# Sixteen of the 128 weighted expert sums of tile 0, moved from TensorE to VectorE

## What is computed

```python
wgt = softmax(best_s) * gelu(h . u[expert])      # 128 weights per token
out = sum over the 128 experts of wgt * v[expert]  # v[expert]: 1024 numbers
x = x + gate2 * out                                # then the last norm
```

## Time and profile before

| | us |
|---|---|
| median of 3 runs (lowest, highest) | 1479.16 (1478.48, 1480.18) |
| the profiled execution on the device | 1486.33 |
| its span, first to last instruction | 1484.4 |
| TensorE busy / VectorE / ScalarE / GpSimd | 1354.0 / 841.1 / 292.7 / 429.6 |
| gathers | 256, 268.48 MB, 43.7% of the DMA engines' span |
| mean granted TensorE clock | 0.983 |

### The profile page before, as it was taken

The page is one execution under the profiler, slowest core; times in us unless marked ns, Lnnn a source line. Parts: engine busy times, 40 slices in busy tenths (PEclk is TensorE's granted clock), DMA queues, the critical chain, the costliest instruction groups (busy, mean ns, idle before and its releaser), DMA issues.

```text
span 1484.4 us, 14879 instructions
## 1 busy us (share of the span) xinstructions
PE 1354.0 (91%) x5314; PEld 872.2 (59%) x5314; DVE 841.1 (57%) x1997; ACT 292.7 (20%) x690; POOL 429.6 (29%) x545
## 2 busy tenths in 40 slices
PE   7999999999999999999988989998989778778776
PEld 6887888898767777667566554444543222222222
DVE  3558451235127667524256567776766767666654
ACT  2023101031010000114423214541221112111101
POOL 0002000120101000000004544564557555655551
PEclk9999999999999999999898998999999999999999
DMA  8343633311557888537339998999999999999995
GB/s 293 115 170 114 227 114 113 120 51 57 171 186 282 309 297 293 204 127 284 113 114 364 423 422 332 395 421 424 424 424 425 425 425 425 425 426 424 425 425 229
DMA packets 119193, 424.52 MB, mean 286 GB/s; under 512 B 10642, under 2 KB 34632, under 8 KB 84176
## 3 DMA queue, kind: packets, MB, share of 16 engines
q0 software_dynamic: 36896, 268.48, 43.7%
q1 hardware_dynamic: 82224, 155.09, 29.0%
HBM read 422.48 MB, written 1.06 MB: 285 GB/s over the span
## 4 chain that ended last, share of the span: by engine, by line
PE 54%; DMA 26%; issue 7%; POOL 7%; ACT 3%; DVE 3%; SPq 0%; POOLq 0%; DVEq 0%; ACTq 0%
PE psum L560 30%; DMA arena<-peer_uv,arena 15%; DMA wr<-peer_uv,arena 7%; PE psum L811 4%; PE psum L1027 3%; POOL wr L2397 3%; POOL arena L2369 2%; DMA xc<-peer_uv,arena 2%; PE psum L787 2%; PE psum L881 1%; PE psum L857 1%; POOL arena L2397 1%; PE psum L608 1%; PE psum L998 1%; PE psum L1045 1%
## 5 line engine op out<-in xcount | busy, mean ns | idle before, releaser
L560 PE MATMUL psum<-hT,wr 128*128 128x256 f32 x1792 | 393.6, 382 | 1.6 <-DVE hT L1583 1.6
L560 PEld LDWEIGHTS psum<-hT,wr 128*128 128x128 f32 x1792 | 342.3, 191 | 51.9 <-issue 5.3
L1027 PE MATMUL psum<-wr,arena 128*128 128x512 f32 x644 | 312.2, 616 | 54.0 <-POOL arena L2369 53.8
L2215 DVE CUSTOM_DVE_ANT_0 wr<-psum,wr 128x1024 f32<-128x1024 f32 x161 | 196.9, 1223 | 148.4 <-DMA wr<-peer_uv,arena 148.3
L1027 PEld LDWEIGHTS psum<-wr,arena 128*128 128x128 f32 x644 | 114.1, 193 | 232.5 <-issue 232.1
L2397 POOL DMA_INDIRECT wr<-peer_uv,arena x161 | 160.8, 999 | 270.0 <-DVE arena L2163 125.4
L1027 PE MATMUL psum<-arena 128*128 128x512 f32 x276 | 135.3, 617 | 27.3 <-POOL arena L2369 27.0
L2369 POOL TENSOR_SCALAR arena<-cst,arena 128x128 f32<-128x128 f32 x256 | 121.8, 476 | 124.7 <-ACT arena L1431 117.1
L1431 ACT ACTIVATE arena<-arena 128x1 f32<-128x1 f32 x256 | 51.0, 202 | 492.8 <-DVE arena L2215 492.3
L1027 PEld LDWEIGHTS psum<-arena 128*128 128x128 f32 x276 | 48.0, 192 | 112.6 <-issue 112.4
L2215 DVE CUSTOM_DVE_ANT_0 arena<-psum,arena 128x1024 f32<-128x1024 f32 x69 | 84.5, 1224 | 50.2 <-DMA arena<-peer_uv,arena 50.1
(11 more groups left out here) (321 smaller groups left out, 1458.7 us busy)
## 6 DMA issues: line engine op xcount, KB each, us to landing
wr<-in_w_in SPq DMA_DIRECT2D x22, 2048.0 KB, 8.4
arena<-in_w_ada SPq DMA_DIRECT2D x12, 2048.0 KB, 9.8
wr<-in_w_up SPq DMA_DIRECT2D x22, 1024.0 KB, 8.0
arena<-piece SPq DMA_DIRECT2D x16, 1024.0 KB, 9.1
wr<-in_w_down SPq DMA_DIRECT2D x5, 2048.0 KB, 9.2
wr<-in_w_a_out SPq DMA_DIRECT2D x2, 2048.0 KB, 8.1
wr<-in_w_b_out SPq DMA_DIRECT2D x2, 2048.0 KB, 8.3
wr<-in_w_o SPq DMA_DIRECT2D x2, 2048.0 KB, 7.7
```

The costliest lines, as they stand in the source:

```text
L560: mm = nc.tensor.matmul(bank[p % 4][:, f * S:(f + 1) * S], slot(i)[:, k, c:c + P], act[:, k, :], start=k == 0, stop=k == KT - 1)
L1027: mm = nc.tensor.matmul(bank[(6, 0)[t] + half][:, :], diag[:, n % DIAGS, :], gring[slot_of][:, D + half * BANK:D + (half + 1) * BANK], sta ...
L2215: V.tensor_tensor_reduce(gring[slot_of][:, 0:D], h2[t], gring[slot_of][:, 0:D], 1.0, 0.0, ALU.mult, ALU.add, dots[:, t, c:c + 1]).then_inc ...
```

## The change

Sets 8, 14, 20, ... 98 (every sixth, 16 in all) get no diagonal and no matmuls. Three sets later, behind the dot of set n + 3, VectorE forms the product of the two weights (128x1) and adds weight times v to a sum in SBUF, `row_sum` (the first time it only writes it). The slot's next gather waits for that (`row_used`). At set 164 VectorE adds `row_sum` to banks 6 and 7 and then goes on as before. The counts of `diag_done` and `pe_used` go by the sets left on TensorE. The room for `row_sum` comes from the `C_SEL` blocks: the table is 1024 columns narrower, and L952 reads one column of the identity 128 times in their place. Every diagonal waits for `norm_done`, not only the first of each 16.

```diff
@@ constants
-C_SEL = C_NEG + NT * S
-C_IOTA = C_SEL + H * P
+C_IOTA = C_NEG + NT * S
...
-    for h in range(H):
-        t[h, C_SEL + h * P:C_SEL + (h + 1) * P] = 1.0
...
+ON_VECTOR = tuple(range(8, 104, 6))
+
+
+def on_tensor(n):
+
+    return n - sum(m < n for m in ON_VECTOR)
...
+        row_sum = sb("row_sum", [P, D])
+        row_weight = sb("row_weight", [P, 1])
@@ tensor
-                        mm = nc.tensor.matmul(o[:, c], cst[0:H, C_SEL + h * P:C_SEL + (h + 1) * P], small[:, 6, 0:n],
+                        mm = nc.tensor.matmul(o[:, c], cst[0:H, C_ID + h:C_ID + h + 1].to_broadcast([H, P]), small[:, 6, 0:n],
                                               start=False, stop=True, skip_group_check=True)
...
+                    if n in ON_VECTOR:
+                        continue
...
-                    pe.wait_ge(s["diag_done"], n + 1)
+                    pe.wait_ge(s["diag_done"], on_tensor(n) + 1)
                     for half in range(2):
-                        mm = nc.tensor.matmul(bank[(6, 0)[t] + half][:, :], diag[:, n % DIAGS, :],
+                        mm = nc.tensor.matmul(bank[(6, 0)[t] + half][:, :], diag[:, on_tensor(n) % DIAGS, :],
@@ vector
+            def vector_sum(n):
+
+                t, c = divmod(n, P)
+                dve.wait_ge(s["gelu_done"], n + 1)
+                chain.wait()
+                chain(V.tensor_tensor(row_weight[:, :], wgt[:, t, c:c + 1], gsoft[:, t, c:c + 1], ALU.mult))
+                chain.wait()
+                row = gring[GATHER[n][0]][:, D:2 * D]
+                i = ON_VECTOR.index(n)
+                if i == 0:
+                    V.tensor_scalar(row_sum[:, :], row, row_weight[:, 0:1], None, ALU.mult).then_inc(s["row_used"], 1)
+                else:
+                    dve.wait_ge(s["row_used"], i)
+                    V.scalar_tensor_tensor(out=row_sum[:, :], in0=row, scalar=row_weight[:, 0:1], in1=row_sum[:, :],
+                                           op0=ALU.mult, op1=ALU.add).then_inc(s["row_used"], 1)
+
+            def add_rows():
+
+                dve.wait_ge(s["pe_used"], on_tensor(P))
+                dve.wait_ge(s["row_used"], len(ON_VECTOR))
+                for n in range(2):
+                    c = slice(n * BANK, (n + 1) * BANK)
+                    V.tensor_tensor(bank[6 + n][:, :], bank[6 + n][:, :], row_sum[:, c], ALU.add).then_inc(s["rows_added"], 1)
...
                     if n == P + 36:
-                        gated_add(0, "pe_used", (P, P), 3, "x_final", (6, 7))
+                        add_rows()
+                        gated_add(0, "rows_added", (1, 2), 3, "x_final", (6, 7))
...
+                    if n - 3 in ON_VECTOR:
+                        vector_sum(n - 3)
@@ gpsimd
             def expert_diagonal(n):
 
+                if n in ON_VECTOR:
+                    return
                 t, c = divmod(n, P)
-                if n >= DIAGS:
-                    pool.wait_ge(s["pe_used"], n - DIAGS + 1)
-                if c % PK == 0:
-                    pool.wait_ge(s["norm_done"], n // PK + 1)
+                i = on_tensor(n)
+                if i >= DIAGS:
+                    pool.wait_ge(s["pe_used"], i - DIAGS + 1)
+                pool.wait_ge(s["norm_done"], n // PK + 1)
...
-                if before is not None:
-                    pool.wait_ge(s["pe_used"], before + 1)
+                if before in ON_VECTOR:
+                    pool.wait_ge(s["row_used"], ON_VECTOR.index(before) + 1)
+                elif before is not None:
+                    pool.wait_ge(s["pe_used"], on_tensor(before) + 1)
```

More of the change, by code:

```diff
@@ L114 @@
 wout_ready x3_done best_done soft_done eid_done gelu_done dot_done
-wuk_zero norm_done diag_done pe_used half_done x_final final_done h2_done""".split()
+wuk_zero norm_done rows_added diag_done pe_used row_used half_done x_final final_done h2_done""".split()
 class Chain:
@@ L2310, in _ @@
                 if n:
-                    dve.wait_ge(s["pe_used"], SETS)
+                    dve.wait_ge(s["pe_used"], on_tensor(SETS))
                 chain(V.tensor_tensor(gated[:, n, :], bank[n][:, :], modb[:, 3, c], ALU.mult))
@@ L2361, in expert_diagonal @@
             def expert_diagonal(n):
+                if n in ON_VECTOR:
+                    return
                 t, c = divmod(n, P)
-                if n >= DIAGS:
-                    pool.wait_ge(s["pe_used"], n - DIAGS + 1)
-                if c % PK == 0:
-                    pool.wait_ge(s["norm_done"], n // PK + 1)
+                i = on_tensor(n)
+                if i >= DIAGS:
+                    pool.wait_ge(s["pe_used"], i - DIAGS + 1)
+                pool.wait_ge(s["norm_done"], n // PK + 1)
                 pool.wait_ge(s["gelu_done"], n + 1)
-                G.tensor_scalar(diag[:, n % DIAGS, :], ident, wgt[:, t, c:c + 1], gsoft[:, t, c:c + 1], ALU.mult,
+                G.tensor_scalar(diag[:, i % DIAGS, :], ident, wgt[:, t, c:c + 1], gsoft[:, t, c:c + 1], ALU.mult,
                                 ALU.mult).then_inc(s["diag_done"], 1)
```

## The result

| | median | lowest to highest | runs |
|---|---|---|---|
| before | 1483.38 us | 1478.48 to 1486.97 | 19 |
| changed | 1488.34 us | 1482.23 to 1493.38 | 19 |

The ratio is 1.0032, 95% interval [1.0019, 1.0045]: by it the changed kernel is 4.7 us slower (the two medians differ by 5.0). The forecast was 3.6 us faster, with a range of up to 1481.5 against a median of 1479.16; on that scale the result is 1483.9. A second measurement of the same kernel gave 1.0031 [1.0012, 1.0051].

What follows compares the result with a forecast made beforehand. Bound by full DMA queues from 820 us, except 891 to 941, where gathers wait for TensorE's sums. Terms -7.2 + 3.6 = -3.6 us gave 1475.6 us against a median of 1479.16; range 1470 to 1481.5.

Steps and rivals of the forecast that it cites:

- The first term: At 891 to 941 us, relieved TensorE lets gathers issue earlier: 7.2 us recovered, ends 0 and 10.3.
- the hole: Stretches 891 to 916 and 916 to 941 us, at 337 and 334 GB/s: 10.3 us of transfer time lost.
- The second term: After 941 us, late vector-summed slots lose 0.75 us at each of gathers 57, 63, 69, 75, 81: 3.6 us.
- the steps of 3.2 us: Sign of being right: dots at 57, 63, 69, 75, 81 about 3.2 us apart, 2.49 between.
- the 390 GB/s in the hole: Sign of being right: 891 to 941 us runs at over 390 GB/s.
- The bound of 7.2: Upper end, in us, of the loss at the five gathers behind vector sums after 941 us; lower end 0.
- Rival 3: Slower: in GpSimd's one queue the vector sum comes late after 941 us; +7 us, 1486, chance 0.14.
- Its point of decision: Rival 3 decides if a sum is done 3 us later than reckoned: lead 1.5, 2.0 us lost per gather.
- Its formula: Into an empty queue a gather takes 6.0 us from issue to dot, so lead L loses 6.0 - 2.5 - L.
- The vector sum's own price: On VectorE behind dot b + 3: 0.16 and 1.28 us; slot free 2.9 us after that dot's start.
- Constants and broadcast weights: Smaller constant table: 0, or a gain of 1.2 us if exposed; weights read 128 times: old 0.19 us a load.
- VectorE's hold on GpSimd: Two-input vector sums lengthen GpSimd issues: at most 12 us over 16 sets, 0 on the path.

Runs made afterwards that it cites:

- e12_again: The changed kernel measured once more, nothing altered; 1.0031 of the kernel before.
- e3_relief: The changed kernel without vector sums: 16 of tile 0's 128 experts left out, their slots free with the dot; 0.9994 of the kernel before.
- e5_early: The changed kernel with the vector sum behind the dot of set n + 1 instead of n + 3; 1.0007 of the kernel before.
- e7_both: e5_early with the diagonal of set b + 2 laid before the wait for vector-summed set b; 1.0015 of the kernel before.
- e13_all: e7_both with ScalarE's copy before unit 0 of tile 1 waiting for the gelu of an earlier set; 1.0002 of the kernel before.
- e15_second: The changed kernel with the vector sum behind the dot of set n + 2 instead of n + 3; 0.9977 of the kernel before.
- e18_second_again: e15_second measured once more, nothing altered; 0.9978 of the kernel before.
- e4_hold: The kernel before with narrower constants, all sums on TensorE; sixteen gathers also wait for the third dot behind their slot's own; 1.0010 of the kernel before.
- e14_hold4: As e4_hold, but the sixteen gathers wait for the fourth dot behind their slot's own; 1.0146 of the kernel before.
- e2_load: The kernel before with narrower constants plus VectorE's sixteen operation pairs on `row_sum` alone, all sums on TensorE, no slot held; 1.0020 of the kernel before.
- e9_psum: e2_load with the long VectorE operation taking one input from PSUM instead of two from SBUF; 1.0001 of the kernel before.
- e8_fill: e3_relief with four zero-weight matmuls, waiting for no diagonal, in place of each dropped sum; 1.0004 of the kernel before.

## Why the prediction was wrong

**The first term, 7.2 us recovered, failed.** Its start came true: in the changed kernel's profile TensorE doesn't stand idle before unit 0 and comes at full clock, and gather 37 goes 3.2 us earlier, counted from dot 12 (forecast: 1.8; 1.2 in e12_again, which stands idle 1.4 us there). Gather 45 went at 913.24 where 914.8 was forecast, but that is luck, since this execution had started 4.0 us better; counted from dot 12 the gather is 4.0 us earlier than before, and 6.4 were forecast. The step that failed is "TensorE then has no 3.54 us to stand idle and keeps its clock ... By set 45 TensorE is 6 us ahead". It took TensorE as the only late one and the wait before unit 0 as its only wait. One step on, in the same unit, TensorE of the changed kernel stands 3.09 us (2.9 in e12_again) until VectorE has masked the logits, where before it stood 0.38:

```profile
884.52 0.70 PE L956 MATMUL psum<-arena 64*128 64x256 f32 x2
...
900.71 1.09 PE L971 MATMUL psum<-cst,arena 128*128 128x128 f32 x4 [3.09 <-DVE amax L2031]
901.59 2.97 PE L1036 MATMUL psum<-xc,arena 128*128 128x512 f32 x4
```

The sum behind it takes 2.97 us and not 1.88, the clock in the two halves of the hole is no better than before (0.89 and 0.90 for 0.88 and 0.93), and gather 49 is back at its old place (0.4 us later, counted from dot 12; in e12_again 0.2 earlier). In e3_relief the wait before unit 0 is longer, 6.68 us, and the full relief of 31 us, with no vector sum at all, gives 0.9994, at best 0.9976. TensorE's attention steps wait for ScalarE and VectorE, whose gelus and dots wait for the gathers. In the three kernels with the late slot the stretch from dot 12 to 49 is 115.9, 116.9 and 118.2 us, mean 117.0, against the 117.1 of the unrelieved kernels: nothing recovered, with an uncertainty of about 1. In the five with an earlier slot (e5_early, e7_both, e13_all, e15_second, e18_second_again) the mean is 115.3: 1.8 us less. But e4_hold, with no relief, has 115.3 too, so even this isn't told from nothing.

**The second term, 3.6 us at the gathers 57 to 81, was too small, and put in the wrong place.** A lead of 4.5 was forecast, and 4.5, 5.2, 4.6 and 4.7 stand in the trace. That the late slot would cost time was right. But the price was taken as 0.75 us at each of these gathers (five of them make 3.8, not 3.6), and their own dots lose 0.2, 0, 1.1 and 0 us, in e12_again nothing at all. The loss falls on the gathers behind them, such as 64 and 65 with 1.2 us each, which wait for TensorE. The term left that out: what a held gather does to the diagonals and sums behind it, and to the clock. Of the signs named, the steps of 3.2 us did not come at these sets (2.7, 2.5, 3.6 and 2.4), nor the 390 GB/s in the hole. From dot 49 to 80 the three kernels take 86.2, 85.5 and 87.4 us, mean 86.4, against 80.9: 5.5 us. 0 + 5.5 = +5.5, and 4.7 were measured. The bound of 7.2 held.

**Rival 3** had the right side and nearly the right size (+7), with the reason half right: the one queue of GpSimd and too short a lead. Its point of decision was not met (it wanted a lead of 1.5, and the leads were 4.5 and more), and none was needed. Its formula, 6.0 - 2.5 - L, would give 0.5 at a lead of 3.0, where 1.8 to 2.9 were lost: the 6.0 us from issue to dot, read from gather 45, is 7.25 in e14_hold4 and 7.2 to 8.1 at these four sets of the changed kernel.

**What held.** The vector sum's own price (0.15 and 1.28 us, slot free 2.9 us after the start of dot b + 3). Constants and broadcast weights: nothing. (Set 164 was not tested alone; e15_second has it and is faster than before.) VectorE's hold on GpSimd is small here, and for the reason given: 3 instructions held, against 11 in e5_early, where the sum comes when GpSimd has other work. The Trainium skill, "SBUF — State Buffer", section "SBUF: two separate sides", has the pair held for a whole instruction and blocking GpSimd operations that read SBUF. The rows agree: in e2_load the sum ends at 998.00 and the issue beside it at 998.86, so 0.86 of its usual 1.0 us comes after the sum. With a PSUM operand (e9_psum) no instruction beside a sum is held, as the page's condition of two SBUF inputs has it.

**What the views should have told.** The 22.8 us that GpSimd waited for sums name the last releaser. They don't say that TensorE, once relieved, would release sooner; for that each of its batches must be followed to what the attention step ahead of it waits for.

## What to carry to other kernels

Where a ring's slots are the limit, count how long before the data are needed a slot comes free, and keep that lead above what the trace shows to be enough (here 5.5 us lost nothing, 4.5 cost 5.5 us over 31 sets, and 3.0 cost 1.8 to 2.9 us at once); in this kernel the moved work paid 0.22% behind the second dot and cost 0.32% behind the third. Relief of the engine that seems late is worth only what its next waits let through: take the work out altogether first to see the size of what can be won (here 0 to 0.2%, where 0.5% was forecast). Among the places that leave enough lead, more than one has to be tried: the first and the second dot differ by 0.3% here for a reason that isn't shown.

## What the runs showed of the hardware

- A DMA share near 1 does not mean the full rate. The changed kernel moves 380 GB/s in 941 to 1016 at a share of 0.99, and the kernel before 421 at 1.01. Where two or three gathers are under way, counted from issues and dots, and not three or four, a tenth of the rate is gone before the share shows it; e14_hold4 has 357 GB/s at 0.95.
- One microsecond of lead has no even price: with leads of 5.5, 4.5 and 3.5 by design (e4_hold, the changed kernel, e14_hold4) the ratios are 1.0010, 1.0032 and 1.0146. (The changed kernel differs from the other two by its relief and its vector sums as well.)
- A gather's issue beside a vector operation with two SBUF inputs is held to about 0.87 us past the end of that operation, 1.74 us instead of 1.00; beside one with an input from PSUM it takes 0.99.
- TensorE's granted clock was lower where it had more free time. In 1016 to 1091 it was 0.98 in the kernel before (busy 69.2 of 75 us), 0.91 in the changed kernel (61.7), 0.88 in e3_relief (58.8), and 0.95 in e8_fill (68.2), where the free time was filled with work. The times of e3_relief and e8_fill don't differ beyond the noise.
